# Splitting a triangular inverse into 32x32 tiles, and filler multiplies ahead of waits

## The reference

```python
a_mat = jnp.where(tri_strict, jnp.einsum('nbhid,nbhjd->nbhij', kb, kc) * decay, 0.0)
t_mat = lax.linalg.triangular_solve(eye + a_mat, jnp.broadcast_to(eye, a_mat.shape),
                                    left_side=True, lower=True, unit_diagonal=True)
u = jnp.einsum('nbhij,nbhjd->nbhid', t_mat, vb)
```

## Time and profile before

| | |
|---|---|
| median of 3 runs | 1694.24 us (1692.28 to 1694.34) |
| the profiled execution | 1694.11 us |
| its span, first to last instruction | 1692.0 us |
| PE busy | 1572.8 us, 93% |
| DVE busy | 1141.4 us, 67% |
| ACT busy | 786.4 us, 46% |
| POOL busy | 115.2 us, 7% |
| mean granted clock of TensorE | 0.964 of 2.4 GHz |

### The profile page before, as it was taken

How to read it: one execution, slowest core, us unless ns; L and a number is a source line. 1 busy time by engine, 2 the same in 40 slices (tenths; PEclk the granted TensorE clock), 3 DMA queues, 4 the chain that set the end, 5 groups by cost and what they waited for, 6 DMA issues and landing times.

```text
span 1692.0 us, 30969 instructions
## 1 busy us (share of the span) xinstructions
PE 1572.8 (93%) x11422; PEld 1380.7 (82%) x11422; DVE 1141.4 (67%) x1913; ACT 786.4 (46%) x1416; POOL 115.2 (7%) x130
## 2 busy tenths in 40 slices
PE   5899978789999999999989999999999889999998
PEld 3687768688777777788778589999898668999997
DVE  5975755554499999967455558885566665477644
ACT  2554543132354444432255457775444445566532
POOL 2000032220200000001000010001000001010000
PEclk8999988899999999999989999999899999999999
DMA  8344420000245555555432034556444223255562
GB/s 355 120 177 156 150 70 2 1 3 1 100 148 178 187 182 187 185 177 170 137 134 88 25 100 162 184 187 212 161 163 147 89 75 99 101 184 186 178 194 90
DMA packets 62906, 230.50 MB, mean 136 GB/s; under 512 B 6816, under 2 KB 8096, under 8 KB 62304
## 3 DMA queue, kind: packets, MB, share of 16 engines
q1 hardware_dynamic: 61408, 223.37, 38.8%
q0 software_dynamic: 1120, 5.54, 1.0%
q10 hardware_dynamic: 288, 0.33, 0.1%
HBM read 228.17 MB, written 1.05 MB: 135 GB/s over the span
## 4 chain that ended last, share of the span: by engine, by line
PE 79%; DVE 11%; ACT 5%; issue 3%; POOL 1%; DMA 1%; DVEq 0%; ACTq 0%; POOLq 0%
PE proj L646 21%; PE proj L648 20%; PE proj L647 20%; DVE w_low L2068 2%; PE bank L698 1%; ACT w_high L1571 1%; PE bank L901 1%; PE bank L918 1%; PE bank L1198 1%; PE bank L921 1%; DVE conv_mid L2148 1%; DMA ident_sb<-ident 1%; PE bank L949 1%; PE proj L1102 1%; DVE mod_products L2199 1%
## 5 line engine op out<-in xcount | busy, mean ns | idle before, releaser
L646 PE MATMUL proj<-h_high,w_high 128*128 128x256 f32 (+1 forms) x1768 | 583.7, 330 | 22.7 <-DVE h_low L2101 14.3
L648 PE MATMUL proj<-h_high,w_low 128*128 128x256 f32 (+1 forms) x1768 | 570.4, 323 | 0.0
L647 PE MATMUL proj<-h_low,w_high 128*128 128x256 f32 (+1 forms) x1768 | 570.1, 322 | 0.0
L2068 DVE TENSOR_TENSOR w_low<-w_raw,w_high 128x1024 fp32r<-128x1024 f32 x322 | 393.1, 1224 | 190.1 <-ACT w_high L1571 188.7
L1571 ACT ACTIVATE w_high<-w_raw 128x1024 fp32r<-128x1024 f32 x322 | 338.2, 1054 | 244.0 <-PE proj L648 240.4
L646 PEld LDWEIGHTS proj<-h_high,w_high 128*128 128x128 f32 x1768 | 335.9, 190 | 65.5 <-issue 18.5
L648 PEld LDWEIGHTS proj<-h_high,w_low 128*128 128x128 f32 x1768 | 336.4, 190 | 27.5
L647 PEld LDWEIGHTS proj<-h_low,w_high 128*128 128x128 f32 x1768 | 335.9, 190 | 25.0
L646 PE MATMUL proj<-act_high,w_high 128*128 128x256 f32 (+1 forms) x608 | 190.4, 313 | 0.4 <-DVE w_low L2068 0.4
L648 PE MATMUL proj<-act_high,w_low 128*128 128x256 f32 (+1 forms) x608 | 189.6, 312 | 0.0
L647 PE MATMUL proj<-act_low,w_high 128*128 128x256 f32 (+1 forms) x608 | 188.9, 311 | 0.0
(11 more groups left out here) (406 smaller groups left out, 1920.5 us busy)
## 6 DMA issues: line engine op xcount, KB each, us to landing
w_raw<-w_stream SPq DMA_DIRECT2D x322, 512.0 KB, 3.3
a_ring<-a_stream SPq DMA_DIRECT2D x80, 512.0 KB, 3.2
a_first<-a_head SPq DMA_DIRECT2D x4, 1024.0 KB, 17.9
a_first<-a_stream SPq DMA_DIRECT2D x4, 1024.0 KB, 18.6
x<-x_in SPq DMA_DIRECT2D x1, 2048.0 KB, 10.5
late_tab<-late_tables POOLq DMA_DIRECT2D x1, 1408.0 KB, 6.6
cond_rows<-cond_rows SPq DMA_DIRECT2D x1, 1024.0 KB, 5.9
cond_rows<-cond_rows POOLq DMA_DIRECT2D x1, 1024.0 KB, 5.1
```

The costliest lines, as they stand in the source:

```text
L646: mm(out_, wh, xh, start=first, stop=False)
L647: mm(out_, wh, xl, start=False, stop=False)
L648: return mm(out_, wl, xh, start=False, stop=last)
L2068: v.tensor_tensor(wl(n), RAW[:, n % 4, :], wh(n), ALU.subtract).then_inc(w_low, 1)
```

## The change

**Levels 0 to 4 on quarters.** The blocks that these levels join are at most 32 wide, so that all they produce lies in the four 32x32 diagonal blocks. `inv_t` and `inv_u_halves` become one tensor `inv_quarters` (both ways round side by side), and each 64x64 matmul becomes two 32x32 ones on the array's diagonal tiles (`QUARTERS`). Level 0 makes both start values by products, and DVE takes them in one subtraction. Levels 1 to 3 have one subtraction on DVE. Level 4 adds the old value in by a second, accumulating matmul with the identity, DVE spreads the result into `inv_u` with a mask (`quarter`), which also writes the zeros that a POOL memset wrote before, and ACT spreads the other way round into `inv_t` (`half`, two activations). From level 5 on the work is as before, with `inv_u` in the place of `inv_u_halves`.

**Fillers.** `keep_busy(n, bank)` issues n f32 matmuls of `ones` by the identity, 128x128 by 128x128, into a bank whose content is not needed; they wait for nothing. They stand ahead of step 0 in both stages (10 and 8), around `out_sums(1)` (7 and 2), in `norm` (3 before the spread and 7 after), around the spread of "mix" (6 and 6), and ahead of the sums of "kv2" (6): 75 in all.

```diff
+            def keep_busy(n, bank_):
+                for _ in range(n):
+                    mm(bank_[:, 0:P], ONES[:], ID[:], start=True, stop=True)
...
-            def norm(name):
+            def norm(name, filler=BK[1]):
                 norm_sum(name)
+                keep_busy(3, filler)
                 norm_spread(name)
+                keep_busy(7, filler)
...
                 pe.wait_ge(G["gb_at"], 7 if st else 4)
                 pe.wait_ge(G["gb_e"], 14 if st else 8)
+                keep_busy(8 if st else 10, BK[0])
...
                     if lev == 0:
                         if k >= 2:
                             pe.wait_ge(G["lv_tu"], at + k - 1)
+                        both = pair_of(b)
                         for h in range(HEADS):
-                            for x in HALVES:
-                                last = mm(out_[x, h, :], CT[x, b, h, :], ID[x, x], start=True, stop=True)
+                            for x, y in zip(QUARTERS, IN_HALF):
+                                mm(both[x, 0, h, :], CT[x, b, h, y], ID[x, x], start=True, stop=True)
+                        for h in range(HEADS):
+                            for x, y in zip(QUARTERS, IN_HALF):
+                                last = mm(both[x, 1, h, :], ID[x, x], CT[x, b, h, y], start=True, stop=True)
+                    elif lev < QLEV:
+                        pe.wait_ge(G["lv_tu"], at + (k - 1 if k < 6 else k - 3))
+                        out_ = heads_of(b, 32)
+                        for h in range(HEADS):
+                            for x, y in zip(QUARTERS, IN_HALF):
+                                last = mm(out_[x, h, :], CT[x, b, h, y], TQ[x, q, 0, h, :], start=True, stop=True)
                     else:
-                        pe.wait_ge(G["lv_tu"], at + (k - 1 if k < 6 else k - 3))
+                        pe.wait_ge(G["lv_tu"], at + k - 3)
+                        if lev == QLEV:
+                            pe.wait_ge(G["lv_t4"], 4 * st + q + 1)
...
+                    if lev < QLEV - 1:
+                        both = pair_of(2 + 2 * b)
+                        for h in range(HEADS):
+                            for x in QUARTERS:
+                                mm(both[x, 0, h, :], TQ[x, q, 1, h, :], M1[x, b, h, 0:32], start=True, stop=True)
+                        for h in range(HEADS):
+                            for x in QUARTERS:
+                                last = mm(both[x, 1, h, :], M1[x, b, h, 0:32], TQ[x, q, 1, h, :], start=True, stop=True)
+                        last.then_inc(G["lv_x"], 1)
+                        return
+                    if lev == QLEV - 1:
+                        out_t, out_u = heads_of(2 + 2 * b, 32), heads_of(3 + 2 * b, 32)
+                        for h in range(HEADS):
+                            for x in QUARTERS:
+                                mm(out_t[x, h, :], TQ[x, q, 1, h, :], M1[x, b, h, 0:32], start=True, stop=False)
+                            for x in QUARTERS:
+                                mm(out_t[x, h, :], TQ[x, q, 1, h, :], ID[x, x], start=False, stop=True)
...
+            keep_busy(7, PL[0])
             out_sums(1)
+            keep_busy(2, PL[0])
             out_spread(1)
...
             norm_sum("final1", 0, 2)
+            keep_busy(6, BK[1])
             pe.wait_ge(n_std, NORM_I["mix"] + 2)
...
+            keep_busy(6, BK[1])
             first_tiles("in2", LAT, SEQ, h_ready("mix"))
...
+            keep_busy(6, BK[5])
             norm_sum("kv2")
...
-                        pool.wait_ge(m_acc, 2 + 2 * MOD_IN)
-                        nc.gpsimd.memset(TU[:], 0.0).then_inc(G["u_zero"], 1)
...
+                    lev, q = LEVELS[k]
+                    if lev < QLEV:
+                        f(M1[:, k % 2, :, 0:32], heads_of(k % 2, 32), ACT.Copy, scale=-1.0 if lev == QLEV - 1 else 1.0).then_inc(G["lv_m1"], 1)
...
+                    if LEVELS[k - 1][0] == QLEV - 1:
+                        act.wait_ge(G["lv_x"], (NSTEP - 4) * st + k - 4)
+                        for c in range(2):
+                            last = f(TT[:, LEVELS[k - 1][1], :, 32 * c:32 * c + 32], heads_of(2 + 2 * ((k - 1) % 2), 32), ACT.Copy, scale=gtab("half", c, 1))
+                        last.then_inc(G["lv_t4"], 1)
...
-                        v.tensor_tensor(TT[:, q, :, :], eye, halves_of(b), ALU.subtract).then_inc(G["lv_tu"], 1)
+                        v.tensor_tensor(TQ[:, q, :, :, :].rearrange("p u h j -> p (u h) j"), eye, pair_of(b).rearrange("p u h j -> p (u h) j"), ALU.subtract).then_inc(G["lv_tu"], 1)
...
-                        if lev < NLEV - 1:
-                            v.tensor_tensor(TT[:, q, :, :], TT[:, q, :, :], halves_of(2 + 2 * b), ALU.subtract)
-                        if lev < NLEV - 2:
-                            last = v.tensor_tensor(TH[:, q, :, :], TH[:, q, :, :], new, ALU.subtract)
+                        if lev < QLEV - 1:
+                            last = v.tensor_tensor(TQ[:, q, :, :, :], TQ[:, q, :, :, :], pair_of(2 + 2 * b), ALU.subtract)
+                        elif lev < QLEV:
+                            last = v.tensor_tensor(TU[:, q, :, :].rearrange("p h (c j) -> p h c j", c=4),
+                                                   heads_of(3 + 2 * b, 32).unsqueeze(2).to_broadcast([P, HEADS, 4, 32]), quarter, ALU.mult)
```

More of the change, by code:

```diff
@@ L49 @@
 NCOLS = _n
-GDN_TABLES = [("cum", 2 * P), ("neg", 2 * P), ("eye", 64), ("lev", 12 * 64)]
+GDN_TABLES = [("cum", 2 * P), ("neg", 2 * P), ("eye32", 32), ("half", 2), ("quarter", 4), ("lev", 12 * 64)]
 LATE_TABLES = [("perm64", P), ("perm32", P), ("cm", SEQ), ("sm", SEQ), ("c64", SEQ), ("s64", SEQ), ("c32", SEQ),
@@ L381, in two_blocks_kernel @@
         TT = place("inv_t", [P, 4, HEADS, 64])
-        TH = place("inv_u_halves", [P, 4, HEADS, 64])
+        TQ = place("inv_quarters", [P, 4, 2, HEADS, 32])
         TU = place("inv_u", [P, 4, HEADS, P])
@@ L633, in last_half, with heads_of, pair_of @@
             return HALVES[1 - q % 2]
+        QUARTERS = [slice(32 * i, 32 * i + 32) for i in range(4)]
+        IN_HALF = [slice(32 * (i % 2), 32 * (i % 2) + 32) for i in range(4)]
+        QLEV = 5
+        def heads_of(b, w):
+            return BK[b][:, 0:HEADS * w].rearrange("p (h j) -> p h j", h=HEADS)
+        def pair_of(b):
+            return BK[b][:, 0:2 * HEADS * 32].rearrange("p (u h j) -> p u h j", u=2, h=HEADS)
         TURNS = [(3, 6), (16, 20)]
@@ L887, in first_product @@
                         pe.wait_ge(G["lv_ct"], (NSTEP - 4) * st + k + 1)
[L888 removed]
+                    out_ = heads_of(b, 64)
                     if lev == 0:
@@ L913, in second_product @@
                         pe.wait_ge(G["lv_tu"], at + k - 1)
-                    out_t, out_u = (BK[i + 2 * b][:, 0:4 * 64].rearrange("p (h j) -> p h j", h=HEADS) for i in (2, 3))
+                    if LEVELS[k - 2][0] == QLEV - 1:
+                        pe.wait_ge(G["lv_t4"], 4 * st + LEVELS[k - 2][1] + 1)
+                    if lev < QLEV - 1:
[15 more added lines that the diff above has]
+                                mm(out_t[x, h, :], TQ[x, q, 1, h, :], ID[x, x], start=False, stop=True)
+                        for h in range(HEADS):
+                            for x in QUARTERS:
+                                mm(out_u[x, h, :], M1[x, b, h, 0:32], TQ[x, q, 1, h, :], start=True, stop=False)
+                            for x in QUARTERS:
+                                last = mm(out_u[x, h, :], ID[x, x], TQ[x, q, 1, h, :], start=False, stop=True)
+                        last.then_inc(G["lv_x"], 1)
+                        return
+                    out_t, out_u = heads_of(2 + 2 * b, 64), heads_of(3 + 2 * b, 64)
                     if lev < NLEV - 1:
@@ L917, in second_product @@
                             for x in HALVES:
-                                mm(out_t[x, h, :], TH[x, q, h, :], M1[x, b, h, :], start=True, stop=True)
+                                mm(out_t[x, h, :], TU[x, q, h, x], M1[x, b, h, :], start=True, stop=True)
                         for h in range(HEADS):
                             for x in HALVES:
-                                last = mm(out_u[x, h, :], M1[x, b, h, :], TH[x, q, h, :], start=True, stop=True)
+                                last = mm(out_u[x, h, :], M1[x, b, h, :], TU[x, q, h, x], start=True, stop=True)
                     else:
```

36 lines of the change are left out of this document (12 added, 24 removed).

## The result

The changed kernel takes 1732.09 us in the median of 4 runs (1724.24 to 1732.19), the kernel before 1694.29 (4 runs). The ratio is 1.0214 with a 95% interval of 1.0185 to 1.0244: 38 us slower, where 14 us faster was predicted, and outside the range.

What follows compares the result with a forecast made beforehand. PE was taken to bound the kernel, busy 93% of the span. Levels -16.0, fillers +3.0, clock -5.4 and +4 summed to -14.4 us from 1694.11, so 1679.7; its own range 1673 to 1686.

Steps and rivals of the forecast that it cites:

- The price of a record: PE's small matmuls in the levels: 8 ns a record on four diagonal tiles, for 29 ns before; bounds 7.3 to 29.
- The other sign that the prediction named for failing: Levels of both stages: the prediction fails if they shrink by less than 10 us in sum.
- The levels on PE: Levels 0 to 4: 2048 records a stage in 16.4 us for 24.4, -16.0 us for both, while PE sets the pace.
- What is late next: Levels 1 to 3: POOL's mask sets a floor of 0.78 us a step; 0.85 taken, so -13.2 us for -15.1.
- rival 3: Levels: DVE's scaling, ACT's squares and POOL's mask set the pace, half the gain left; -5 us, 1689; chance 0.14.
- The clock: PE's clock: fillers holding it give -5.4 us; more idle time in levels 0 to 3, at 0.75, costs +4.
- The fillers: 75 fillers in stage starts, norms and output: mostly covered by PE's waits, +3.0 us net; 16.8 if nothing covered them.
- Case 5: Levels 0 to 4: clock stays low as matmuls use a quarter of the array; +15 to +20 us, 1711; chance 0.06.
- Case 6: Levels: four tiles don't overlap, a record still costs near 29 ns; +70 us, 1765, or +54 at 25 ns; chance 0.08.

Runs made afterwards that it cites:

- burst (c): In the kernel before, ahead of norm n2_1: 1024 unread f32 records on four 32x32 tiles, as a loop of 16 times 64 records; 15.0 us.
- burst (b): In the kernel before, ahead of norm n2_1: 1024 unread f32 records on four 32x32 tiles, 32 columns, written out; 26.1 us.
- (d): In the kernel before, ahead of norm n2_1: 1024 unread f32 records on four 32x32 tiles, as a loop of 4 times 256 records; 12.0 us.
- (a): In the kernel before, ahead of norm n2_1: 1024 unread f32 records on two 64x64 tiles, 64 columns, written out; 29.8 us.

## Why the prediction was wrong

- **The price of a record** was right: 8.4 ns at the full clock for the 8 taken, and 0.43 us for 32, 13 ns, at the half. The other sign that the prediction named for failing came: the levels were to shrink, and levels 0 to 4 took 31 us more in both stages together, where -16 was in the sum.
- **The levels on PE** is the step that failed. It multiplied 2048 records a stage by that price and had 16.4 us; what it lacked was a term for bringing the instructions. 2048 records are 16 blocks, and at 3.4 to 3.9 us a block these are 54 to 62 us a stage. By level: level 4 has 5 blocks, 17 to 20 us, measured 18.3 and 16.7. Levels 1 to 3 have 9, 31 to 35 us, measured 31.5 in the context stage, with 4 us of waits for DVE among them. In the latent stage they took 42.4, and there the supply accounts for 3.0 us of waits and the clock for the most. "As long as PE sets the pace" was the wrong condition: in level 4 neither PE nor another engine did.
- **What is late next** asked only the engines. POOL's 0.78 us a step hardly mattered (one wait of 0.2 us in levels 1 to 4); ACT would have (rival 3), behind the supply.
- **The clock** is the term that was too small. +4 was expected from idle time in the levels, with 0.75 as the value; it was 0.66 and 0.52 in levels 1 to 3, 0.50 and 0.68 in level 4, and not only where PE was idle. Where the supply sets the pace it costs little: 16.90 us for level 4 at 1.00, 18.30 at 0.50, with a block every 3.4 to 3.7 us at the full clock and 3.4 to 3.9 at the half. Where PE has other work it costs in full: 8.9 us in levels 1 to 3 of the latent stage alone.
- **The fillers** were summed at +3.0 and -5.4, so -2.4; on 64x64 tiles all of them gave -3.1, 1689.42 for 1692.55, and the norms' part of it can't be told from nothing. In the changed kernel the 8 at the latent stage were not covered: the step named DVE's first start value as the cover, but the change itself had made level 0 need only POOL's mask. They started at 332.06 and the first product at 335.77, 3.7 us at the half clock. The kernel without any filler took no less, though (1733.62): the time came back elsewhere.
- **Rivals.** None of the six named the supply. Case 5 gave the right sign and named the low clock; that came, as the smaller of the two causes, and at 1711 the case was 21 us short. Its reason isn't shown: small records alone came back to the full clock in burst (c). Case 6's price per record, 25 to 29 ns in the mean, is what the stream came to (27), by another mechanism than tiles that don't overlap. Its argument against itself was right, though the earlier trace rows don't show it: in the trace of before, records on two tiles start 7 ns apart and the next pair 52 ns later.

What stays open: why a block takes 3.4 us or more when its packet itself takes about 1 us in the trace, and how far ahead PE fetches. In burst (b) a packet starts 1.0 to 1.3 us after a block's first record, and PE goes on 1.2 to 1.5 us after it has ended. Open too is what keeps the clock at 0.50 through 22.8 us without a wait. No run put the levels on quarters into a loop, which the bursts suggest as the remedy. Levels 5 and 6 took 1 and 2 us more as well, and that was not looked into.

## What to carry to other kernels

Beside the work of an engine, count its instructions: in these runs a PE stream that was written out got no more than 128 matmul records with their weight loads in 3.4 to 3.9 us, 27 to 30 ns each, so splitting matmuls into smaller ones gains nothing once a record costs that little. Look at how often the instruction queue has a packet in the stretch that you change, and work out how often it will need one. In the bursts the same matmuls as a loop took less than half the time (12.0 us for 26.1). Then look at the granted clock in each stage apart from the waits: other work between the small matmuls pays for it. Fillers that hold the clock belong into a wait, ahead of every semaphore that the next product waits for; behind it they are a delay.

## What the runs showed of the hardware

- A loop of 64 records (128 instructions) or 256 records (512) was not fetched again: one and two packets for 1024 records, and 15.0 and 12.0 us for 26.1. A pass of the loop cost some 0.3 us: at the full clock six passes of (c) took 5.0 us, 0.83 each, where 64 records at 8.5 ns are 0.54. (d) has one wait on issue of 2.1 us in its 12.0.

```profile
1070.00:1075.00 5.00, 4.43 (x384) 3.87 (x380) 0.00 (x0) 0.00 (x0) 0.00 (x0) 1.00 0.00 0
```

- f32 records on four 32x32 tiles start 8.5 ns apart (160 in 1.55 us ahead of the first wait of burst (b), less the 0.19 that the last one takes). The Trainium skill, "TensorE: Matmul & The Clock Gate" (Wait — 56ns, not 53.3ns?), has a floor of about 25 ns from one matmul's start to the next; these start closer, on different tiles.
- With waits for instructions the clock fell as it does with other waits: it was 0.57 in burst (b), 1.00 in (a) and (d), and in (c) 0.50 for the first 2.6 us, with PE busy on small records throughout, then 1.00. In the latent stage of the changed kernel PE was busy with small records and larger work between them for 22.8 us, and it stayed at 0.50.
